# One-core hybrid decoder step: prompt attention in pairs of heads, value products in two column halves, groups turned back, top-k rounds moved

## The reference, cut to what matters

```python
# group A (g = 0): dense causal attention, 8 heads, keys of 64 + 32 dimensions, values of 64
s = (einsum(q_nope, k_nope) + einsum(q_rope, k_rope)) * MLA_SCALE      # masked to k_pos <= q_pos
o = softmax(s) @ v
# group B (g = 1): for each query the 128 best keys by an indexer score, then attention over them
sc = where(k_pos <= q_pos, index_scores(qi, w, k_idx), -inf)
_, sel = top_k(sc, 128)                       # 512 // 4
s = einsum(q, k[sel]) * DSA_SCALE + rel_bias[t5_bucket(q_pos - sel)]
o = softmax(s) @ v[sel]                       # 8 query heads, 2 key and value heads (4 queries each)
# then per-group RMS norm of o, the output projection, and a SwiGLU FFN
```

## Time and profile before

| | us |
|---|---|
| median of 3 runs | 1182.32 |
| the profiled execution | 1180.58 |
| its span, first to last instruction | 1178.8 |
| mean granted TensorE clock | 0.987 of full |
| PE busy | 1143.9 |
| DVE busy | 681.6 |
| ACT busy | 404.4 |
| POOL busy | 101.3 |

### The profile page before, as it was taken

The page is one execution under the profiler, slowest core; times in us unless marked ns, Lnnn a source line. Parts: engine busy times, 40 slices in busy tenths (PEclk is TensorE's granted clock), DMA queues, the critical chain, the costliest instruction groups (busy, mean ns, idle before and its releaser), DMA issues.

```text
span 1178.8 us, 22158 instructions
## 1 busy us (share of the span) xinstructions
PE 1143.9 (97%) x9006; PEld 1008.9 (86%) x9006; DVE 681.6 (58%) x1533; ACT 404.4 (34%) x802; POOL 101.3 (9%) x155
## 2 busy tenths in 40 slices
PE   7999999998999999999999999999999999999998
PEld 5898986465587899999999877579999999999998
DVE  4545845735889787778886633464544545453440
ACT  4523224532477655555555423431101010100000
POOL 3100002001204500000000011100000000000000
PEclk9999999987999999999999999999999999999999
DMA  9996641022102202211124276623333333243340
GB/s 320 275 274 185 198 126 54 1 72 59 49 1 82 82 1 81 81 74 32 59 81 135 90 252 230 232 73 91 95 96 94 89 89 89 71 129 92 99 120 28
DMA packets 141875, 129.16 MB, mean 110 GB/s; under 512 B 17635, under 2 KB 135824, under 8 KB 139712
## 3 DMA queue, kind: packets, MB, share of 16 engines
q1 hardware_dynamic: 137184, 86.78, 25.2%
q0 software_dynamic: 4608, 41.23, 9.6%
HBM read 124.58 MB, written 3.41 MB: 109 GB/s over the span
## 4 chain that ended last, share of the span: by engine, by line
PE 81%; DVE 9%; ACT 4%; DMA 3%; issue 3%; SPq 0%; POOL 0%; ACTq 0%; DVEq 0%; POOLq 0%
PE psV L1254 21%; PE psV L1001 13%; PE psA L1254 11%; PE psA L669 8%; PE psV L1122 4%; PE psV L938 3%; PE psV L962 2%; PE psA L981 2%; PE psV L800 2%; DVE msk L1961 1%; PE psV L701 1%; PE psA L1051 1%; DVE top L1960 1%; PE psA L949 1%; PE psA L1087 1%
## 5 line engine op out<-in xcount | busy, mean ns | idle before, releaser
L1001 PE MATMUL psV<-r_r,wide_r 128*128 128x260 f32 x1536 | 207.5, 288 | 3.3 <-DVE msk L2194 2.9
L1001 PEld LDWEIGHTS psV<-r_r,wide_r 128*128 128x128 f32 x1536 | 190.4, 189 | 5.9 <-issue 3.3
L1552 ACT ACTIVATE wring<-psV 128x512 f32<-128x512 f32 x128 | 76.2, 597 | 91.4 <-PE psV L1001 69.0
L1254 PE MATMUL psV<-qiz_r,wring_r 128*128 128x260 f32 x528 | 93.9, 283 | 0.0
L2393 DVE TENSOR_TENSOR wide<-wide,psV 128x520 f32<-128x520 f32 x22 | 15.3, 696 | 125.0 <-PE psV L1254 125.0
L2195 DVE TENSOR_REDUCE msk<-wring 128x8 f32<-128x512 f32 x128 | 86.4, 676 | 0.0
L1254 PEld LDWEIGHTS psV<-qiz_r,wring_r 128*128 128x128 f32 x528 | 76.2, 188 | 0.0
L669 PE MATMUL psA<-wide_r,wring_r 128*128 128x260 f32 x416 | 76.1, 285 | 0.0
L1254 PE MATMUL psA<-qiz_r,wring_r 128*128 128x260 f32 x352 | 70.9, 283 | 0.0
L1254 PE MATMUL psA<-qiz_r,r_r 128*128 128x260 f32 x352 | 70.9, 282 | 0.0
L1254 PE MATMUL psA<-hT_r,r_r 128*128 128x260 f32 x352 | 70.8, 283 | 0.0
(11 more groups left out here) (565 smaller groups left out, 2576.4 us busy)
## 6 DMA issues: line engine op xcount, KB each, us to landing
wring<-w_ffn_in SPq DMA_DIRECT2D x44, 512.0 KB, 3.8
wide<-w_ada SPq DMA_DIRECT2D x11, 1024.0 KB, 6.6
wring<-w_ffn_out SPq DMA_DIRECT2D x16, 704.0 KB, 4.7
tok<-w_ada SPq DMA_DIRECT2D x9, 1024.0 KB, 5.4
wring<-w_in SPq DMA_DIRECT2D x24, 256.0 KB, 5.8
wring<-w_out SPq DMA_DIRECT2D x8, 512.0 KB, 6.6
wide<-w_out SPq DMA_DIRECT2D x2, 2048.0 KB, 8.1
r<-w_ada SPq DMA_DIRECT2D x3, 1024.0 KB, 10.7
```

The costliest lines, as they stand in the source:

```text
L1001: mm = pe.matmul(kx[m % 2][:, hf, :], w, wtab[:, b % 2, l, 2 * k + hf, :], start=(k == 0 and w is high and l == 0), stop=(k == 1 and w is ...
L1254: mm = pe.matmul(out[:, hf, 0:HT], w[:, k, :], x[:, hf * HT:(hf + 1) * HT], start=(k0 + k == 0 and x is xh and w is high), stop=(k0 + k == ...
L1552: A(sq2[m % 2].rearrange("p (x n) -> p x n", x=2), kx[m % 2][:, :, 0:256], ACT.Square).then_inc(kx_squared, 1)
```

## The change

- **Pairs.** Within a group the heads go in the order 0, 4, 1, 5, 2, 6, 3, 7, and PE works on pairs (i, i+4): iteration p does the two score products of pair p+1, the transposes of pair p, and the value products of pair p-1. In group B both score products wait until DVE has read both scores of the pair before.
- **Values stationary.** In a value product 64 columns of values are now stationary and 128 turned probabilities are streamed; head i writes partitions 0 to 63 of the bank and head i+4 partitions 64 to 127 (the two column halves of the array). One ACT copy takes the transposes of both heads.
- **Turned back.** The output now has the value dimension in its partitions. So after each group DVE copies the bank to SBUF (`copy_group`), PE transposes its four blocks (`turn_back`), and `take_group` scales them as before, two entries later. For the last group this falls into the samples' first pages.
- **Rounds moved.** 8 top-k rounds run while the bias rows make their round trip, 15 before the new token's keys are taken, 16 in the place of the 22, and 9 after odd entries to 17 (the mask is cut after entry 19).
- **Search spread.** The same 29 pieces, after even entries from 16 to 56; PE's eight sums in iterations 12, 14 to 26.
- **Smaller:** the root of the squares moves from before the first page to the third, its inverse to the fourth; several semaphores are merged, so that the first bias product also waits for `ohf`. The score products have the same operands as before, with 96 rows in group A and 128 in group B.

```diff
-        AT = [(g, qt, h) for g, qt in GROUPS for h in range(H)]
+        AT = [(g, qt, h) for g, qt in GROUPS for h in (0, 4, 1, 5, 2, 6, 3, 7)]
-        half_steps = lambda u: 0 if u < 51 else 1 if u < 56 else 3
-        STEP_AT = [55 + k for k in range(9)]
         KA = 8
+        COUNT_AT = [12 + 2 * k for k in range(KA)]
+        half_steps = lambda u: 0 if u % 2 or u < 16 or u > 24 + 4 * KA else 1 if u <= 24 or u % 4 == 0 else 2
...
+            def score_pair(p):
+                g, qt, i = AT[2 * p]
+                n, qs, W = V_S + 2 * p, slice(qt * 128, (qt + 1) * 128), (qt + 1) * 128
+                if g == 0:
+                    pair = [(qcat[0:QK, i + 4 * e, qs], kcat[0:QK, i + 4 * e, 0:W]) for e in range(2)]
+                else:
+                    pair = [(qz[:, i + 4 * e, qs], kT[:, 0:W]) for e in range(2)]
+                    pe.wait_ge(v_free, n)
+                for e, (lhs, rhs) in enumerate(pair):
+                    if g == 0:
+                        pe.wait_ge(v_free, n + e - 1)
+                    pe.matmul(sv(n + e)[:, 0, 0:W], lhs, rhs, start=True, stop=True).then_inc(v_full, 1)
+            def turn_pair(p):
+                pe.wait_ge(pt_taken, p)
+                for e in range(2):
+                    u = 2 * p + e
+                    pe.wait_ge(exp_done, u + 1)
+                    for kt in range(AT[u][1] + 1):
+                        mm = pe.transpose(psA[:, 0, e, kt * 128:(kt + 1) * 128], sP[:, u % 3, kt * 128:(kt + 1) * 128], ident)
+                    mm.then_inc(pt_full, 1)
+            def value_pair(p):
+                g, qt, i = AT[2 * p]
+                x = p // 4
+                pe.wait_ge(pt_taken, p + 1)
+                if x >= 2 and p % 4 == 0:
+                    pe.wait_ge(o_copied, x - 1)
+                for kt in range(qt + 1):
+                    for e in range(2):
+                        h = i + 4 * e
+                        vv = vm[:, kt, h * 64:(h + 1) * 64] if g == 0 else tok[:, kt, 416 + e * 64:480 + e * 64]
+                        mm = pe.matmul(psV[64 * e:64 * e + 64, x % 2, 1, i * 128:(i + 1) * 128], vv,
+                                       sPT[:, (2 * p + e) % 4, kt * 128:(kt + 1) * 128], start=(kt == 0), stop=(kt == qt), skip_group_check=True)
+                mm.then_inc(pv_done, 2)
+            pe.wait_ge(a_free, A_IP + 16)
+            for p in range(-1, NP + 1):
+                if p + 1 < NP:
+                    score_pair(p + 1)
+                if p == -1:
+                    sample_scores()
+                if p in COUNT_AT:
+                    count_total(pe, COUNT_AT.index(p)).then_inc(cnt_total, 1)
+                if p >= 6 and p % 4 == 2:
+                    turn_back(pe, p // 4 - 1)
+                if 0 <= p < NP:
+                    turn_pair(p)
+                if p == NP:
+                    pe.wait_ge(pt_taken, NP)
+                    latent_turn(pe, 0)
+                if p >= 1:
+                    value_pair(p - 1)
...
+        def turn_back(pe, x):
+            pe.wait_ge(o_copied, x + 1)
+            pe.wait_ge(o_free, x)
+            for i in range(4):
+                mm = pe.transpose(o_by_pair(x)[:, i * 128:(i + 1) * 128], oS[x % 2][:, i * 128:(i + 1) * 128], ident)
+            mm.then_inc(o_turned, 1)
...
                 if m < 2:
-                    pe.wait_ge(o_free, len(AT) // 8 - 1 + m)
+                    pe.wait_ge(o_copied, len(AT) // 8 - 1 + m)
                 expand(m)
+                if m == 0:
+                    turn_back(pe, 7)
+                if m == 1:
+                    pe.wait_ge(o_free, 8)
...
-                if 1 <= u <= NA:
-                    n, W = A_PT + u - 1, (AT[u - 1][1] + 1) * 128
-                    act.wait_ge(a_full, n + 1)
-                    if u - 1 >= 3:
-                        act.wait_ge(pv_done, u - 3)
-                    A(sPT[:, (u - 1) % 3, 0:W], sa(n)[:, 0, 0:W], ACT.Identity).then_inc(a_free, 1)
+                if u >= 2 and u % 2 == 0:
+                    w = u - 2
+                    W = (AT[w][1] + 1) * 128
+                    act.wait_ge(pt_full, w + 2)
+                    if w >= 4:
+                        act.wait_ge(pv_done, w - 2)
+                    A(sPT[:, w % 4:w % 4 + 2, 0:W], psA[:, 0, :, 0:W], ACT.Identity).then_inc(pt_taken, 1)
...
-            EARLY = 22
-            ROUND_AT = list(range(8)) + [8, 10, 11, 13, 15] + [8 * x + y for x in range(2, 6) for y in (1, 4, 6)] + [48, 50]
+            ROUND_AT = list(range(1, 20, 2))
...
             v.tensor_scalar(g8, sv(V_BIAS)[0:8, 0, 0:384], -1.0, None, ALU.mult).then_inc(v_free, 1)
+            for _ in range(8):
+                next(rounds)
...
+            for _ in range(15):
+                next(rounds)
             v.wait_ge(v_full, V_KN + 1)
...
-            for _ in range(EARLY):
+            for _ in range(16):
                 next(rounds)
...
+            def copy_group(x):
+                v.wait_ge(pv_done, 8 * x + 8)
+                v.tensor_copy(oS[x % 2], psV[:, x % 2, 1, :]).then_inc(o_copied, 1)
...
-                if u >= 8 and u % 8 == 3:
-                    take_group(u // 8 - 1)
+                if u >= 13 and u % 8 == 5:
+                    copy_group(u // 8 - 1)
+                if u >= 15 and u % 8 == 7:
+                    take_group(v, u // 8 - 1)
```

More of the change, by code:

```diff
@@ L311, in build @@
         kx = [psV[:, x, :, 0:260] for x in range(2)]
-        lps = [psA[:, (A_PT + x) % 2, 0, :] for x in range(2)]
+        lps = [psA[:, x, 0, :] for x in range(2)]
+        o_by_pair = lambda x: psA[:, 1, 0, :] if x < 7 else psA[:, 0, 1, :]
+        oS = [hT[:].rearrange("p a t -> p (a t)")[:, 1024 + x * 512:1536 + x * 512] for x in range(2)]
         krps, ropeps, latp = psA[:, 0, 1, :], psA[:, 1, 1, 0:128], psA[:, 1, 1, 0:256]
@@ L421, in build @@
         y_stored = [sem(f"y_stored{s}") for s in range(2)]
-        qs_gained, w1_ready, irel_ready, wz_ready, pn_ready = (sem(x) for x in (
-            "qs_gained", "w1_ready", "irel_ready", "wz_ready", "pn_ready"))
-        far_loaded, mask_ready, top_done = (sem(x) for x in ("far_loaded", "mask_ready", "top_done"))
-        idx_pages = [sem(f"idx_pages{x}") for x in range(2)]
-        mla_pages = [sem(f"mla_pages{x}") for x in range(2)]
+        queries_ready, new_ready = sem("queries_ready"), sem("new_ready")
+        pt_full, pt_taken, o_copied, o_turned = (sem(x) for x in ("pt_full", "pt_taken", "o_copied", "o_turned"))
+        mask_ready, top_done = sem("mask_ready"), sem("top_done")
+        pages_in = [sem(f"pages_in{x}") for x in range(2)]
+        IDX_IN = 16 * NB // 2
         kv_rows = [sem(f"kv_rows{x}") for x in range(3)]
@@ L537, in sp_program @@
             sp.dma_start(rbias, a["rel_bias"]).then_inc(bias_loaded, 16)
-            sp.dma_start(ohf, a["k_onehot"][:, 384:384 + PAST + 1]).then_inc(far_loaded, 16)
+            sp.dma_start(ohf, a["k_onehot"][:, 384:384 + PAST + 1]).then_inc(bias_loaded, 16)
             sp.wait_ge(v_free, V_BIAS + 1)
@@ L1525, in act_program, with square_mix @@
             latent_high(act, 0)
-            square_mix(7)
             act_decode(act)
             act_tail(act)
+        def square_mix(act, x):
+            act.wait_ge(o_free, x + 1)
+            nc.scalar.activation(dump, otm[x], ACT.Square, accum_out=ss8[:, x:x + 1]).then_inc(o_squared, 1)
         def latent_high(act, p):
@@ L1606, in act_decode @@
                 square(m)
+                if m == 1:
+                    square_mix(act, 7)
+                if m == 2:
+                    act.wait_ge(o_squared, 8)
+                    A(ss8, ss8, ACT.Sqrt, scale=1.0 / 512, bias=epsc[:]).then_inc(mix_root, 1)
                 if j == 1:
@@ L2114, in dve_program @@
             steps = search()
-            def take_group(x):
-                v.wait_ge(exp_done, 8 * x + 8)
-                v.reciprocal(rsum, lsum[x % 2]).then_inc(l_free, 1)
-                v.wait_ge(l_free, x + 1)
+            def copy_group(x):
                 v.wait_ge(pv_done, 8 * x + 8)
-                v.tensor_tensor(heads(otm[x]), heads(psV[:, x % 2, 1, :]), rsum.unsqueeze(2).broadcast_to([128, H, 64]), ALU.mult).then_inc(o_free, 1)
-            NA = len(AT)
+                v.tensor_copy(oS[x % 2], psV[:, x % 2, 1, :]).then_inc(o_copied, 1)
             for u in range(NA):
@@ L2150, in dve_program @@
             low_part(v, 0)
-            take_group(7)
+            copy_group(7)
             dve_decode(v, link, steps, mask_bias)
@@ L2162, in table, with take_group @@
                 v.tensor_tensor(low, w, high.bitcast(F32), ALU.subtract).then_inc(tab_done, 1)
+        def take_group(v, x):
+            v.wait_ge(exp_done, 8 * x + 8)
+            v.reciprocal(rsum, lsum[x % 2]).then_inc(l_free, 1)
+            v.wait_ge(l_free, x + 1)
+            v.wait_ge(o_turned, x + 1)
+            v.tensor_tensor(otm[x].rearrange("p (e i d) -> p e i d", e=2, i=4), o_by_pair(x).rearrange("p (i e d) -> p e i d", i=4, e=2),
```

(5 more changed lines are left out.)

89 lines of the change are left out of this document (25 added, 64 removed).

## The result

The changed kernel took **1176.21 us** (median of 7 runs, 1170.44 to 1177.67), the kernel before 1184.01 beside it (7 runs): ratio **0.9929**, interval 0.9909 to 0.9949. In a second series the ratio was 0.9937 (0.9918 to 0.9956) with a median of 1176.03. The profiled execution took 1176.45 us, with a span of 1174.6 and a mean clock of 0.981.

What follows compares the result with a forecast made beforehand. PE was taken to bound the long groups, with DVE's chain nearly as binding in the short ones. -7.4 + 1.8 + 1.3 - 1.0 + 0.5 = -4.8 us against the median 1182.32 gave 1177.5 us, range 1171.5 to 1183.5.

Steps and rivals of the forecast that it cites:

- Overlap of the halves: Value products on PE: column halves run side by side, 0.053 us an instruction, 0.213 us per key tile for a pair.
- halves take turns: Rival, value products: no overlap, costing 15.4 us, 1193 us in all; within the 0.14 chance of slower cases.
- Switch 0.30 per pair: PE going from full-width products to half tiles and back: 0.30 us for each of 32 pairs, bounds 0 and 0.4.
- switch hidden: Rival, PE's mode changes: 0.25 us saved in each of 16 long pairs, 4 us more gain, 1173.5 us; chance 0.12.
- Long groups -7.4 and the four turns in them: Groups with four and three key tiles: pairs save 0.57 and 0.35 us, -7.4 us; four output turns there or later, +1.8.
- Rounds moved at 0: Top-k rounds moved into DVE's idle stretches before the attention: both batches fit, cost 0; without the cover, 1 us.
- Short groups +1.3: Four groups with one or two key tiles, DVE's chain and turns: +1.3 us together, bounds -1 and +4.
- list of signs: What would show the forecast in the trace; for the short groups, lengths of 9.6, 7.4, 7.4, 9.6 us.
- lockstep rival: Pairs tie PE to the second of two DVE entries, eating the gain: 1180.7 us, +1.6 at worst; chance 0.24.
- Start -1.0: Attention's start: second score goes ahead of the sample scores, one score product leaves the queue; -1.0 us, between 0 and -2.
- End +0.5: Last pair to the samples' pages, with a wait for `take_group` and ACT's table load: +0.5 us, between -0.5 and +2.
- DVE's idle stretches: Sign before 251 and 277 us: DVE's idle time shrinks to under 2 us, PE's stage before 306.7 unchanged.

Runs made afterwards that it cites:

- experiment 3: Changed kernel with value products as before (probabilities stationary, full width), pairs, copies and turns kept: 1184.96 us, ratio 1.0009 to the kernel before.
- experiment 2: Changed kernel with both heads of a pair writing the same 64 partitions, so one column half is used: 1188.96 us, ratio 1.0044 to the kernel before.
- experiment 4: Changed kernel with one tiny half-array product ahead of each pair's transposes, one more switch per pair: 1184.21 us, ratio 0.9984 to the kernel before.
- Experiment 5: Kernel before with only the top-k rounds moved as in the change: 1177.84 us, ratio 0.9930 to the kernel before.
- experiment 8: Changed kernel, each group B score product waiting only until the entry before it has been read: 1172.74 us, ratio 0.9913 to the kernel before.
- experiment 6: Changed kernel with the 22 and 26 rounds at their old places: 1191.47 us, ratio 1.0048 to the kernel before.
- experiments 9 to 12: Changed kernel, search moved to the last two groups (1177.42 us; with free group B scores 1171.78) or each piece one entry later (1175.54; with free scores 1175.25).

## Why the prediction was right, and where it was not

The forecast was 1177.5 us and the result 1176.21. The direction was right, and so were the costs of the pair. That the time came so close is partly luck. The change was -7.8 us, 3.0 more than the forecast -4.8; 1.7 of this does not show in the time, because the kernel before had a median of 1184.01 beside it and not the 1182.32 that I added to. And two large effects in the short groups, -3.8 and +3.8, cancelled each other.

- **Overlap of the halves, 0.053 us an instruction: right.** The pair with four key tiles takes 3.82 us, forecast 3.81, and 4.39 with values as before (experiment 3), forecast 4.38. The table in experiment 2 gives 0.055. The rival *halves take turns* is ruled out by experiment 2: its 12.5 us in the sum and 1.7 in the first stretch are the 15.4 that it was priced at, within 1.2. The page "TensorE: Matmul & The Clock Gate" of the Trainium skill, Part 3, lets weight loads overlap running products only if their row groups differ. The 16 products on two column halves in 1.03 us, with all 128 rows in each, disagree: each half takes a new product every 0.11 us, the time in which 128 columns stream, so a load per product was hidden.
- **Switch 0.30 per pair: right.** The terms show it: scores 1.83 for 1.78, transposes 0.96 for 0.88, values 1.03 for 0.85, together 0.31 (by the table 0.15 of the 0.18 in the values is paid once, the rest goes with their number). The rival *switch hidden* falls by the same rows, and experiment 4 puts 0.35 on one more visit. The page "TensorEngine Tiling (Array Packing)" of the Trainium skill, Tiling Modes, says that a change of mode drains the engine; the trace agrees in the direction and gives the price, which the page doesn't.
- **Long groups -7.4 and the four turns in them: right in the sum, not in each group.** By the stretches at full clock: first -2.3 for -3.3 with the start's -1.0 in it, second -1.1 for -1.0, seventh -0.6 for -1.0, eighth to page 0 -2.7 for -1.8. The seventh and the eighth differ from the forecast since I had left the search's sums on PE out of the long groups. In the kernel before all eight stood behind entry 55, 0.14 us each and the last 0.24, 1.2 us in the eighth stretch; two of them are now in the seventh group:

```profile
388.83 0.28 PE L970 MATMUL psA<-wring,mats 128*128 128x8 f32 x2
388.97 0.53 PE L949 MATMUL psA<-mats,r 128*128 128x128 f32 x3
```

- **Rounds moved at 0: the step that failed.** I priced only what the rounds cost where they go to, and took their cover there as the whole question. What they freed where they came from had no term of its own: my cycles for the short groups counted them as gone, and the gain stood only in a bound ("-1, rounds gone from the short groups pay"). Experiment 5 gives **-4.3 us** for the move alone: -3.8 in the short groups, -0.6 in the seventh, and +0.1 in the last. The rows for it were there: DVE busy for 88 to 92% of the short groups at PE idle of 1.0 and 1.5 us, and a chain with a round of 1.5 us in it.
- **Short groups +1.3: 0.0 measured, as -3.8 and +3.8.** The four last 33.7 us after and before. My own cycles, four pairs each of 2.4, 1.8, 1.8 and 2.4 us, add up to 33.6, which is 0 and not +1.3; the list of signs has 34.0, and the rest of the term had no row behind it. Against experiment 5 they are 3.8 longer: 1.8 by the lockstep (experiment 8, 31.95), some 1.8 by the four turns (0.44 each) and the rest by the pieces, the last two not measured alone. The lockstep rival was thus right as a mechanism: waits of 3.2 us, 2.3 of them real by experiment 8. Its time of 1180.7 was wrong since the rounds paid for it. Part of this was in my cycle for k=1 (1.8 us a pair, measured 7.15/4 = 1.79); for k=2 in group B I had 2.4 and it took 2.55, the chain's worst case that stood in the bound.
- **Start -1.0: not found as such.** The second score product does go ahead of the sample scores, but PE waits 0.53 us for DVE before it. In the execution at full clock the next pair's scores start 4.21 us after the first score; before, the second score had run by 3.60 + 0.91 = 4.5 us, with some clock lost, so at most 0.3 us was gained. The saving of the whole stretch is 2.3, and I had assumed the clock to be down in both; it was down in one of two executions after, which is worth 3.4 us.
- **End +0.5 and the eighth turn: +0.3 from page 0 to page 4, for +0.9.** The wait that I named is there, 0.44 for 0.6, ahead of the rope turns:

```profile
405.87 1.69 PE L1031 MATMUL psV<-r_r,wide_r 128*128 128x260 f32 x12
408.00 0.66 PE L1061 MATMUL psA<-mats,wide 128*128 128x128 f32 x4 [0.44 <-DVE qiz L2206]
```

- **DVE's idle stretches: right.** The 8.59 and 18.57 us are now 1.58 and 0.72, each behind the rounds, and the stages before 306 are longer by no more than they vary between executions of one kernel (242.37 and 245.82 us for the same instruction in two of before).

```profile
254.92 1.23 DVE L2011 COPY wring<-psV 128x1024 f32<-128x1024 f32 x1 [1.58 <-PE psV L857]
...
280.40 0.15 DVE L2046 TENSOR_SCALAR small<-psV 8x8 f32<-8x8 f32 x1 [0.72 <-PE psV L898]
```

**The change taken apart.** From the kernel before to the one with moved rounds -4.3 us in the sum. From there to pairs with turns, spread search and lockstep, but full-width values (experiment 3), +5.6: eight turns by 0.44 are 3.5 and the lockstep is 2.3, which together is about that (an estimate; the two were not taken out of that kernel). Then the halves, -5.5. So behind the start the attention's new form pays for itself and no more, in this order of steps; the gain in the sum is that of the moved rounds, and the first stretch adds its 2.3. In the other order the pairs, with the search spread, lose (experiment 6). What stays open is why one execution keeps its clock at the start and another doesn't, and how much of the longer seventh group in experiments 9 to 12 is DVE's own work and how much its waits.

## What to carry to other kernels

When work is moved off a busy engine, price the place that it leaves as well as the place where it goes: here that was worth 4.3 us, two thirds of the net gain at full clock, and a term of zero hid it. A product with 64 columns streamed against 128 stationary is worth turning round into column halves where it comes in long runs, at about 0.3 us per visit and with the output's turning back to pay. When pairs are formed, wait for the buffer that is needed, not for the pair: that one line was worth 2.3 us, and moving DVE's small pieces about was worth nothing here. Where a piece waits for another engine, look at what stands behind it in both lists before moving it.

## What the runs showed that I had not expected

- The granted clock at the attention's start falls in some executions and not in others of the same kernel, after the same instructions: 14.42 or 17.79 us for one stretch. A pair of profiled executions (-4.1 us) can so stand far from the medians (-7.8).
- Value products on half the array with nothing beside them are not slower each than at full width: 16 take 1.89 us against 1.74 in experiment 3, but the 0.15 is there with 4 as well (0.58 against 0.40), and four more cost 0.44 us in both.
- A switch is paid on both sides and three operations long: in the value part (0.15 to 0.18), in the transposes (0.08 to 0.09) and in the scores (0.05).
